# Five edits to a fused decoder block: recurrence tail, gate sums, out-projection loads, last token tile, expert choice

## The reference

```python
h = modulate(rmsnorm(x, g_norm_mix[l]), sh_m, sc_m)
z = h @ w_in[l]                       # rwkv | latent attention | two gates of 1024
y_rwkv = rwkv7_branch(z_rwkv, ...)    # recurrence, 8 heads of 64; head norm; bonus; * g
y_mla = mla_branch(z_mla, ...)        # causal attention, 8 heads
gate_rwkv, gate_mla = jnp.split(jax.nn.sigmoid(z_gates), 2, axis=-1)
merged = gate_rwkv * (y_rwkv @ w_branch[l, 0]) + gate_mla * (y_mla @ w_branch[l, 1])
x = x + gt_m[:, None, :] * (merged @ w_out[l])
h2 = modulate(rmsnorm(x, g_norm_ffn[l]), sh_f, sc_f)
x = x + gt_f[:, None, :] * hier_moe(h2, ...)  # best of 4 groups, then best 2 of its 8 experts
```

## Time and profile before

| what | value |
|---|---|
| median of 3 runs | 1576.92 us (1576.4 to 1578.83) |
| the profiled execution | 1577.04 us |
| its span | 1575.2 us |
| mean granted TensorE clock in it | 0.945 of full speed |
| TensorE busy | 1389.8 us, 88% of the span |
| VectorE busy | 768.5 us, 49% |
| ScalarE busy | 496.0 us, 31% |
| GpSimd busy | 257.8 us, 16% |
| traffic | 246.54 MB, 157 GB/s on average |

### The profile page before, as it was taken

One profiled execution on the slowest core, in us unless ns is written; L12 is line 12 of the kernel. 1 busy time (PEld: TensorE's weight loads), 2 busy tenths in 40 slices (PEclk: granted clock), 3 DMA queues, 4 the chain that ended last, 5 costly groups with the idle time before them and its releaser, 6 DMA issues. The chain is left out here.

```text
span 1575.2 us, 32797 instructions
## 1 busy us (share of the span) xinstructions
PE 1389.8 (88%) x14309; PEld 996.4 (63%) x14309; DVE 768.5 (49%) x1095; ACT 496.0 (31%) x906; POOL 257.8 (16%) x301
## 2 busy tenths in 40 slices
PE   3799999976999998799988999998994899999990
PEld 0597777734899988677766888786883433333330
DVE  0644866756666664544656555555435211211215
ACT  1543332353344443444544445222111111111110
POOL 0001222205556542011110000000000111111110
PEclk7899999996999999899998999999996799999995
DMA  9841222270000020650021113414018599999958
GB/s 357 295 138 47 81 74 74 67 268 2 4 4 4 4 64 4 177 198 14 15 92 69 54 54 135 173 40 154 39 40 338 218 355 413 414 420 411 410 220 322
DMA packets 80636, 246.54 MB, mean 157 GB/s; under 512 B 8680, under 2 KB 41960, under 8 KB 63728
## 3 DMA queue, kind: packets, MB, share of 16 engines
q1 hardware_dynamic: 73152, 227.69, 38.9%
q0 software_dynamic: 7344, 16.79, 2.8%
HBM read 216.12 MB, written 38.29 MB: 162 GB/s over the span
## 5 line engine op out<-in xcount | busy, mean ns | idle before, releaser
L2807 PE MATMUL ps<-gu,xT 128*32 128x512 f32 x1536 | 175.9, 599 | 1.4 <-ACT xT L2888 0.7
L2807 PEld LDWEIGHTS ps<-gu,xT 128*32 128x32 f32 x1536 | 47.7, 111 | 106.3 <-issue 102.3
L3022 DVE TENSOR_TENSOR sg<-sg,ps 128x256 f32<-128x256 f32 x25 | 10.5, 422 | 211.2 <-ACT sg L2893 211.2
L351 PE MATMUL ps<-hh,wr_h 128*128 128x512 f32 x224 | 93.1, 416 | 0.6 <-DVE wr_l L347 0.6
L352 PE MATMUL ps<-hl,wr_h 128*128 128x512 f32 x224 | 88.5, 395 | 0.0
L353 PE MATMUL ps<-hh,wr_l 128*128 128x512 f32 x224 | 88.4, 395 | 0.0
L2825 PE MATMUL ps<-dn,hidT 128*32 128x512 f32 x768 | 86.8, 592 | 0.5 <-ACT hidT L2897 0.5
L2016 DVE TENSOR_REDUCE nmax<-ps 128x1 f32<-128x896 f32 (+4 forms) x64 | 45.8, 753 | 71.2 <-PE ps L1914 70.6
L1402 DVE TENSOR_TENSOR inverses<-inverses,ps 128x512 f32<-128x512 f32 (+1 forms) x80 | 49.9, 631 | 62.2 <-PE ps L1625 61.9
L1187 POOL TENSOR_TENSOR off<-mats,cst 128x256 f32<-128x256 f32 x80 | 65.8, 839 | 56.6 <-PE ps L1609 56.5
L1625 PE MATMUL ps<-inverses,xx 64*64 64x64 f32 x1280 | 71.2, 218 | 0.0
(11 more groups left out here) (411 smaller groups left out, 3338.5 us busy)
## 6 DMA issues: line engine op xcount, KB each, us to landing
gu<-w_e_gate SPq DMA_DIRECT2D x34, 1024.0 KB, 12.8
gu<-w_e_up SPq DMA_DIRECT2D x34, 1024.0 KB, 15.3
dn<-w_e_down SPq DMA_DIRECT2D x34, 1024.0 KB, 11.6
wbuf<-w_ada SPq DMA_DIRECT2D x16, 1024.0 KB, 11.4
wbuf<-w_ada SPq DMA_DIRECT2D x16, 512.0 KB, 6.1
wraws<-w_gates SPq DMA_DIRECT2D x16, 512.0 KB, 4.9
rows<-expert_rows SPq DMA_DIRECT2D x16, 512.0 KB, 9.3
wr<-w_rwkv SPq DMA_DIRECT2D x14, 512.0 KB, 3.6
```

What stands on the lines that cost most here:

```text
L351: nc.tensor.matmul(out, wt[0], mov[0], start=(k == 0), stop=False)
L2807: last = nc.tensor.matmul(ps[part, GB[b]], xT[:, b, k, part], gu[:, expert(m, c_) % WB, :, k], start=(k == 0), stop=(k == KD - 1))
```

## The change

Five places are edited. (1) Recurrence: `part` gets four slots, `turned(6)` and `turned(7)` use banks of their own, `turned(0)`, `turned(1)`, `turned(2)` stand later in period 7 on TensorE, `affine(4)` earlier on ScalarE, `finished(5)` later on VectorE; the load of the first attention pair waits for the last `wu` product. (2) Gates: `T3` is computed before the factors of pair 1, and the splits of the second to fourth sums stand later. (3) The loads for the out-projection: `scf` before the branch products end, `gt` ahead of `x1`, `x1` in four pieces with a semaphore each, the small ones behind the first piece. (4) The last token tile is done in two halves of 512 columns on TensorE, VectorE and ScalarE. (5) Group and experts of tiles 0 to 3 are chosen behind tiles 4 and 5, the others at the end; the one-hot operands of line 2774 are f32r instead of f32; `idx` is computed before the table of extra blocks, and the load of the last `gt` waits for that table (`tb_s`).

```diff
-            part = kT[:, 5].rearrange("p (b c n) -> p b c n", b=2, c=CT)
+            part = kT[:, 5:7].rearrange("p a (b c n) -> p (a b) c n", b=2, c=CT)
+            PARTS = part.shape[1]
-            TURN = tuple(IB_ for IB_ in ((6, 7), (6, 7), (6, 7), (0, 1), (6, 7), (0, 1), (6, 7), (0, 1)))
-            USED = (None, 0, 1, None, 2, 3, 4, 5)
+            TURN = ((6, 7), (6, 7), (6, 7), (0, 1), (6, 7), (0, 1), (4, 5), (2, 3))
+            USED = {1: 0, 2: 1, 4: 2, 5: 3}
+                    sp.wait_ge(sm["wu"], NT * PER["wu"])
                     load_pair(sp, 0)
...
                         if j == NT:
                             roots(2)
+                            affine(4)
...
-                    affine(4)
                     squares(NT - 1)
...
                     finished(4)
-                    finished(5)
                     spread(7)
                     guarded(3)
                     inverted(3)
                     normal(7)
+                    finished(5)
                     finished(6)
...
                 sum_low(0)
-                for j in (P1, P5):
-                    factor_low(1, j)
+                dve.wait_ge(v_kept, 16 * CT)
+                nc.vector.tensor_tensor(T3[:, 0], h22, h12, ALU.subtract).then_inc(t_sum, 1)
+                factor_low(1, P1)
                 dve.wait_ge(t_sum, 2)
                 nc.vector.tensor_tensor(h21, h21, T2[:, 0], ALU.subtract).then_inc(t_sum, 1)
+                factor_low(1, P5)
+                dve.wait_ge(t_sum, 4)
                 sum_low(1)
-                dve.wait_ge(v_kept, 16 * CT)
-                nc.vector.tensor_tensor(T3[:, 0], h22, h12, ALU.subtract).then_inc(t_sum, 1)
-                sum_low(2)
...
                     factor_low(i, P6)
+                    if i == 1:
+                        sum_low(2)
                     factor_low(i, P2)
-                    if i == 1:
-                        sum_low(3)
...
+                    if i == 1:
+                        sum_low(3)
                     factor_low(i, P4)
...
+                sp.wait_ge(mod_out, 16 * 2 * CH)
+                sp.dma_start(scf[:], mod_dram[:, 4 * D:5 * D].broadcast_to([P, D])).then_inc(mods, 16)
                 sp.wait_ge(b_mm, 2 * KD)
-                sp.dma_start(x1[:], x[0].rearrange("(t p) d -> p t d", p=P)).then_inc(x_in7, 16)
...
                 sp.dma_start(gt, mod_dram[:, 2 * D:3 * D].broadcast_to([P, D])).then_inc(gt_in, 16)
+                for j in range(NT // 2):
+                    two = slice(2 * j, 2 * j + 2)
+                    sp.dma_start(x1[:, two], x_rows[:, two]).then_inc(x_in7[j], 16)
+                    if j == 0:
...
+                        sp.dma_start(numbers, route[:, RCOL["iota"][0]:RCOL["iota"][0] + NE]).then_inc(mods, 16)
...
+                    for halves in ((0, 1),) if t < NT - 1 else ((0,), (1,)):
+                        for k in range(KD):
+                            if t and (halves[-1], k) == (1, 6 if t < NT - 1 else 3):
+                                row_transposes(t - 1)
...
+                    if t == CT:
+                        dve.wait_ge(lg_s, CT)
+                        best_group(early, slice(0, CT))
+                    if t == CT + 1:
+                        best_experts(early, slice(0, CT))
...
+                def last_tile(t):
+                    both_halves = [slice(n * 512, (n + 1) * 512) for n in range(2)]
...
+                    for n, at in enumerate(both_halves):
+                        dve.wait_ge(o_mm, t + 1 + n)
+                        nc.vector.tensor_tensor(tmp[:, at], ps[:, 2 * (t % 2) + n], gt[:, at], ALU.mult).then_inc(o_ev, 1)
...
+                        nc.vector.tensor_tensor(x1[:, t, at], x1[:, t, at], tmp[:, at], ALU.add).then_inc(o_add, 1)
...
+                best_group(link, slice(CT, NT), ge)
+                best_experts(link, slice(CT, NT), ge)
...
-            row_is = alias("row_is", [P, 2, NT, P], f32)
+            row_is = alias("row_is", [P, 2, NT, P])
-            block_is = alias("block_is", [P, 2, NT, NPASS + 2], f32)
+            block_is = alias("block_is", [P, 2, NT, NPASS + 2])
...
-                sp.wait_ge(idx_s, 1)
+                sp.wait_ge(tb_s, 1)
```

More of the change, by code:

```diff
@@ L1721, in turned @@
                         pe.wait_ge(yn, t + 1)
[L1722 to L1726, removed]
+                        if t in USED:
+                            pe.wait_ge(aff, CT * (USED[t] + 1))
+                            pe.wait_ge(fin, 2 * (USED[t] + 1))
+                        elif t == 3:
                             wait("wu_ev", NT - 1, 2)
+                        elif t == 6:
+                            wait("y_ev", NT - 1, 1)
+                        elif t == 7:
+                            wait("st_ev", NT - 1, 2)
                         for c_ in range(CT):
@@ L1775, in _ @@
                             half_products(j, 3)
+                        if j == NT - 1:
+                            turned(1)
                         if step(q):
@@ L1792, in _ @@
                             half_products(j, 4)
+                        if j == NT - 1:
+                            turned(2)
                         if step(n):
@@ L2081, in build @@
             h2 = YTM[:, 0:3]
+            at_, parts = NT * (NG + NE), []
+            for shape in ((2, NT, NE), (1, NT, NG), (1, NT, NG), (4, NT, 1), (1, NT, 1), (1, 1, NE)):
+                n = shape[0] * shape[1] * shape[2]
+                parts.append(YTM[:, 3, at_:at_ + n].rearrange("p (a t e) -> p a t e", a=shape[0], t=shape[1]))
+                at_ += n
+            hot, group, g1, m1, gsum, numbers = (v if v.shape[1] > 1 else v[:, 0] for v in parts)
+            m1, gsum, numbers = m1[:, :, :, 0], gsum[:, :, 0], numbers[:, 0]
@@ new lines, in build, with first_hot, wide @@
+            lg_group, lg_expert = lg[:, :, 0:NG], lg[:, :, NG:]
+            def first_hot(link, dst, vals, peak, least, n):
+                tiles = dst.shape[1]
+                count = numbers[:, 0:n].unsqueeze(1).broadcast_to([P, tiles, n])
+                def wide(ap):
+                    return ap.unsqueeze(2).broadcast_to([P, tiles, n])
+                link(nc.vector.tensor_tensor(dst, vals, wide(peak), ALU.not_equal))
+                link(nc.vector.scalar_tensor_tensor(dst, dst, 1000.0, count, ALU.mult, ALU.add))
+                link(nc.vector.tensor_reduce(least, dst, AX.X, ALU.min))
+                link(nc.vector.tensor_tensor(dst, count, wide(least), ALU.is_equal))
@@ L2103, in build @@
             raw_in = slots(st, "raw_in7", 2)
+            x_in7 = slots(st, "x_in7", NT // 2)
+            x_rows = x[0].rearrange("(t p) d -> p t d", p=P)
             y_in = slots(st, "y_in7", CT)
@@ L2269, in row_transposes @@
                     for g in range(2):
+                        pe.wait_ge(h2_s, u + 1 + (g if u == NT - 1 else 0))
                         for j in range(4):
@@ L2580, in logits @@
                     nc.vector.tensor_tensor(lg[:, u], ps[:, 6, 0:NG + NE], br_[:], ALU.add).then_inc(lg_s, 1)
-                for t in range(NT):
+                for t in range(NT - 1):
                     dve.wait_ge(o_mm, t + 1)
@@ L2635, in build @@
             e1, e2, both, beyond, rank = (each[:, i] for i in range(5))
-            hot = each[:, 5:7]
             sel, upto = (each[:, i].rearrange("p t e -> p (t e)") for i in (2, 7))
```

175 lines of the change are left out of this document (97 added, 78 removed).

## The result

Before 1576.7 us, after 1559.3 us (medians of four runs each, 1576.1 to 1578.8 and 1558.6 to 1561.0): ratio 0.9889, 95% interval 0.9872 to 0.9906. The change makes the kernel 17 us faster. The prediction had the sign, but said 27 us, and its range ended at 1558.0. The profiled execution of after took 1559.73 us, with a span of 1557.9.

The account below looks back on a forecast made before the run. TensorE, busy 88% of the span, was taken as the bound from the first gather on, so cuts ahead of it shift the rest. 4.2 + 1.5 + 9.0 + 7.7 + 2.4 + 1.9 + 3.0 - 2.4 = 27.3 us off 1577.04: 1549.7, range 1544.5 to 1558.

Parts of the forecast that it names:

- recurrence, period 7 and end: Recurrence: shorter TensorE waits in period 7 save 4.2 us (bounds 2 to 5.2), the reordered end 1.5 (0 to 2.5).
- first pair's load, moved: End of recurrence: first attention pair's load, issued some 20 us ahead of its use, costs nothing; without that cover attention starts later.
- gates: Gates: moving T3 earlier lets P6 start almost at once, saving 9.0 us (bounds 5 to 9.7).
- out-projection loads: Out-projection: earlier loads bring tile 0's `h2` sooner and avoid the lower clock, saving 7.7 us (bounds 6.9 to 7.8).
- last tile and choice: Out-projection's end: last tile in halves saves 2.4 us (1.5 to 4.8), early choice of experts 1.9 (1.5 to 2.2).
- slots: Line 2774's matmuls: 16 f32r instructions instead of 32 take 4.0 us instead of 7.07, saving 3.0 (2.5 to 4).
- gather: First expert gather: issued among queued expert weights, it takes 7.0 us instead of 4.60, losing 2.4 (bounds 0 to 4.4).
- not half: Rival, recurrence and gates: they give about half, 8 us instead of 14.7, as other producers become late; 1556.4 us, chance 0.14.
- the queue's end: Rival, first gather: it waits out the weights' backlog and lands at 1233.6 instead of about 1229.8; 1553.5 us, chance 0.18.
- the last tile ran at the lower clock: Last tile: logits stay at 3.65 us; the rival, full clock kept, saves 2.4 us more, 1547.3 us, chance 0.12.
- the weights of the passes: Rival, expert passes: weights become the bound and each of 17 passes lengthens; 1.9 us each gives 1582 us, chance 0.02.
- if f32r had the fast weight load: Slots: with short f32r weight loads they would take 2.2 us plus a few tenths, saving 4.5 us instead of 3.0.

## Why the prediction was off by ten microseconds

The sum said 27.3 us. Per term, with the means of the profiles that have the edit and those that don't:

| term | predicted | measured |
|---|---|---|
| recurrence, period 7 and end | 4.2 + 1.5 | 6.6 |
| first pair's load, moved | 0 | -3.3 |
| gates | 9.0 | 8.2 |
| out-projection loads | 7.7 | 7.2 |
| last tile and choice | 2.4 + 1.9 | 3.9 |
| slots | 3.0 | 3.0 |
| gather | -2.4 | -4.4 |
| attention, untouched (first profiles) | none | -3.5 |

The lines without the last give 21.2 us, which would be 1555.8, inside the range; with it 17.7, and the spans of the first profiles part by 17.3. The last line is that of one pair of profiles. By the ratios the changed kernel saved 17.5 us (0.9889) and, measured again, 19.6 (0.9876), so 1.6 to 3.7 us less than the terms give; where these go in the medians is not shown.

**The step that failed** is this one: "so I cost it at nothing. If that cover were gone attention would start that much later." I looked for the cover of the load at its far end, whether the pair would be there in time, and it was: attention began at once. The cost was at its near end. While the load's 2 MB are under way TensorE's next block of instructions comes late, wherever the load is issued, and in the last period of the recurrence, on the path that sets the end, nothing hides a hole of 3.8 us, and the clock falls behind it. At its old place the load made a hole of 3.1 us too. In the old order the two places cost the same: the late load added 5.5 us behind the last `wu` copy (26.1 against 20.6) and took off 6.5 ahead of it, at the means (ratio 1.0008). In the new order it added 6.3 behind it (24.9 against 18.7, means) and took off only 3.0 ahead: 3.3 us lost (233.1 against 229.8 for the stage). So the new order takes up part of an early hole, so that moving it away saves less than the late hole costs. By the whole runs the loss is larger, 6.6 and 4.6 us (0.9847 against 0.9889 and 0.9876). The kernel with the load put back, 1553.0 us, lies 3.3 us above the forecast and inside its range. The sizes in that passage of the prediction were off too, without effect: the pair is 2 MB, not 1.8, and its last transfer landed 10.3 us after its issue, not 7.4, at 628 us, still 13 us ahead of attention. The trace of before had the row, 3.1 us of TensorE at line 1712 until "issue", and I did not read it, because I looked at waits with a named releaser only.

**The gather** was a term of the right kind and the wrong size: 7.0 taken, 8.7 to 9.0 measured in five profiles with the full queue, 4.2 to 4.6 in the six with the old tail, 4.4 to 4.5 in three with a queue made empty. The bound of 4.4 on the loss held it; my reason for the middle, that "only its first part is disturbed", has nothing for it: it took what a gather among full queues takes. The rule cited from the Trainium skill, "DMA: Bandwidth & Descriptors", section "Issuing engines are not separate DMA queues", that transfers interleave whichever engine started them, is borne out by the queues' rows of after, 1215 to 1217 us (packets, MB, share): GpSimd's gather (q0) and SyncE's weights (q1) share the engines up to the gather's landing at 1216.5, and weights still come behind it.

```profile
q1 hardware_dynamic: 94, 0.48, 58.0%
q0 software_dynamic: 93, 0.32, 39.4%
```

It shares from its first packet on, but that packet itself comes later: 4.5 us after the issue in the five profiles with the full queue, 1.9 to 2.0 in the nine others. So of the 4.4 us that the full queue costs some 2.6 pass ahead of the first packet, and 1.8 in the transfer.

**Attention.** The prediction took unchanged stages as unchanged. The second profile of the same program shows that one of them is worth 3.5 us one way or the other in a single execution, and the first profile of before had drawn the good lot. But it is not the whole rest: in the second profiles of before and after attention took 171.8 and 172.3 us, and the spans still part by 17.2 (1573.6 and 1556.4). There it is mostly the recurrence that differs from the table, 234.4 against 233.8 us, because that profile of before has the shortest of the old order. A single pair of profiles leaves some 3 us open in the stages, and a range around 1549.7 needed that much more to each side.

**What held.** No failed rival explains the miss: recurrence and gates gave 14.8 for the 14.7 said, before the load's cost, not half; the gather did not wait for the queue's end, though it landed only 2 to 3 us ahead of it; the last tile ran at the lower clock (3.64 us for the logits) as forecast; the table's rows were hidden. `turned(1)` waited 1.3 us (0.9 said), P6 started without a wait, tile 0 lost nothing at line 2332, the slots end 4.1 us after they start (4.0 said), and the weights of the passes were waited for 0.6 us. The slots also settle how the other rule from the Trainium skill, "TensorE: Matmul & The Clock Gate", section "Weight-path perf modes", that a fast weight load applies where the type is not FP32, is to be read for f32r: if f32r had the fast weight load, 4.5 us would have been saved; it was 3.0, so f32r doesn't count as such a type here, and a weight load of line 2880 took 333 ns at the median, exactly what the f32 one took the earlier trace rows.

**Open** is why the clock falls behind the same 2.34 us wait in one execution and not in the other, and why the low part at the first gate tile is 1.1 us late in some; no run was made for either. Open too is what makes the median of after 1.6 to 3.7 us slower than the terms.

## What to carry to other kernels

Where you place a large transfer, ask what else comes through the same engines while it runs: TensorE with its 24 small matmuls a microsecond (269 in the 11 us ahead of the hole of before) took in a block of instructions every 3.5 to 3.9 us, and a "<- issue" wait inside a loop without semaphores is the sign that it didn't come. Cut such a transfer into pieces, as here of 0.5 to 0.75 MB, issued 15 and 32 us apart, or try other places for it; the runs here don't tell the two remedies apart (0.9834 and 0.9847). And before you delay a transfer to clear the way for another, list all that stands behind it on its queue: here the wait for a row of 4 KB, broadcast, took back all of a gain of 4.4 us.

## What the runs showed of the hardware that was not expected

- TensorE stood 2.8 to 4.0 us with nothing to wait for, beginning 5 to 9 us after a transfer of 2 MB was issued, in eleven profiles of nine kernels with the load in one piece; the hole went where the load was issued, and in the three kernels with the load in three pieces the longest such wait took 0.81 to 1.27 us.
- In all eleven a 16 KB transfer of the instruction queue, 9.2 to 11.9 us behind the one before it, started within 1.4 us of the hole's beginning and ended 1.3 to 1.5 us ahead of the hole's end.
- The granted clock fell to 0.67 over 10 us at such a hole at the end of the recurrence (621 to 631 us in after), and was 1.00 over the 10 us ahead of it; at the hole of before (581 to 591 us) it stayed 1.00.
- The same program's attention took 175.7 us in one execution and 172.3 in another; the instructions are the same and the granted clock is what differs.
- A gather of 0.5 MB took 4.2 to 4.6 us when the weights' queue had run out or nearly so, its first packet 1.9 to 2.0 us after the issue, and 8.7 to 9.0 among weight loads, its first packet after 4.5.
- The weight load of an f32r operand took as long as that of an f32 one: 333 ns at the median in lines 2880 and 2774, both at the lower clock.
